# Attention on one core: the next pair's q and k turned in steps one and two, masked bias rows for each query tile

## What is computed

```python
def _fox_attend(q_blk, c_q, pos_q, k, v, c_k, pos_k):
    s = jnp.einsum('bhqd,bhkd->bhqk', q_blk, k).astype(jnp.float32) * (FOX_HEAD_DIM ** -0.5)
    s = s + (c_q[..., :, None] - c_k[..., None, :])
    s = jnp.where(pos_k[None, :] <= pos_q[:, None], s, -jnp.inf)
    p = jax.nn.softmax(s, axis=-1)
    return jnp.einsum('bhqk,bhkd->bhqd', p, v.astype(jnp.float32))
...
    o = o * jax.nn.sigmoid(gate.astype(jnp.float32))
```

## Time and profile before

| | us |
|---|---|
| median of 3 runs | 1462.0 (1460.33 to 1466.8) |
| the profiled execution, its time | 1460.39 |
| its span, first to last instruction | 1458.6 |
| PE busy in the span | 1385.2 (95%) |
| DVE, ACT, POOL busy | 532.5, 524.5, 476.3 |
| the attention steps within the span | 215.3 to about 330 |
| mean granted TensorE clock | 0.992 of full |

### The profile page before, as it was taken

One profiled execution on the slowest core, in us unless ns is written; L12 is line 12 of the kernel. 1 busy time (PEld: TensorE's weight loads), 2 busy tenths in 40 slices (PEclk: granted clock), 3 DMA queues, 4 the chain that ended last, 5 costly groups with the idle time before them and its releaser, 6 DMA issues. The chain is left out here.

```text
span 1458.6 us, 26900 instructions
## 1 busy us (share of the span) xinstructions
PE 1385.2 (95%) x11180; PEld 1037.7 (71%) x11180; DVE 532.5 (37%) x1383; ACT 524.5 (36%) x1096; POOL 476.3 (33%) x457
## 2 busy tenths in 40 slices
PE   7999998889999999999989999999999999888986
PEld 6788876567788888888867787776666665555553
DVE  3102118761312200212153613355464464444435
ACT  4325438772422222222246532333332222222222
POOL 5334546434544444444455755320000000000000
PEclk9999999999999999999999999999999999999999
DMA  5133221004232223330232131659999999999995
GB/s 187 65 111 115 88 72 47 31 16 147 84 102 71 87 87 115 116 115 15 101 124 97 58 116 59 238 196 390 403 418 420 419 420 419 420 419 420 419 419 208
DMA packets 83899, 286.49 MB, mean 196 GB/s; under 512 B 8764, under 2 KB 31456, under 8 KB 59200
## 3 DMA queue, kind: packets, MB, share of 16 engines
q1 hardware_dynamic: 83376, 283.60, 50.0%
q0 software_dynamic: 288, 1.05, 0.2%
q10 hardware_dynamic: 112, 0.09, 0.0%
HBM read 282.59 MB, written 2.13 MB: 195 GB/s over the span
## 5 line engine op out<-in xcount | busy, mean ns | idle before, releaser
L491 POOL TENSOR_TENSOR wring_halves<-wring,wring_halves 128x512 fp32r<-128x512 f32 x274 | 356.9, 1307 | 376.9 <-ACT wring_halves L486 375.1
L486 ACT CAST wring_halves<-wring 128x512 fp32r<-128x512 f32 x274 | 168.3, 621 | 433.4 <-PE ps L1207 416.6
L1205 PE MATMUL ps<-wring_halves,big_halves 128*128 128x512 f32 x612 | 241.5, 395 | 4.9 <-POOL wring_halves L491 3.8
L1205 PE MATMUL ps<-hT_halves,wring_halves 128*128 128x512 f32 x480 | 187.4, 390 | 2.4 <-DVE big_halves L1964 2.4
L1206 PE MATMUL ps<-big_halves,wring_halves 128*128 128x512 f32 x480 | 186.8, 389 | 0.0
L1207 PE MATMUL ps<-hT_halves,wring_halves 128*128 128x512 f32 x480 | 186.7, 389 | 0.0
L2654 POOL TENSOR_TENSOR rstd<-rstd,half 128x1 f32<-128x1 f32 (+1 forms) x21 | 13.6, 649 | 505.3 <-DVE rstd L2607 476.6
L1207 PE MATMUL ps<-wring_halves,hT_halves 128*128 128x512 f32 x436 | 170.6, 391 | 0.0
L1206 PE MATMUL ps<-wring_halves,hT_halves 128*128 128x512 f32 x436 | 170.6, 391 | 0.0
L1205 PEld LDWEIGHTS ps<-wring_halves,big_halves 128*128 128x128 f32 x612 | 115.4, 189 | 33.4 <-POOL wring_halves L491 7.3
L1725 PE MATMUL ps<-xn,fixed 128*128 128x512 f32 x256 | 120.0, 612 | 0.4 <-DVE fixed L2402 0.4
(11 more groups left out here) (349 smaller groups left out, 1997.5 us busy)
## 6 DMA issues: line engine op xcount, KB each, us to landing
big<-in_moe_w_dram SPq DMA_DIRECT2D x90, 1024.0 KB, 25.4
wring<-in_moe_w_dram SPq DMA_DIRECT2D x70, 1024.0 KB, 25.5
wring<-in_ffn_w_in_dram SPq DMA_DIRECT2D x22, 1024.0 KB, 7.1
hT<-in_moe_w_dram SPq DMA_DIRECT2D x20, 1024.0 KB, 25.3
wring<-in_fox_w_in_dram SPq DMA_DIRECT2D x7, 2048.0 KB, 8.7
wring<-in_gla_w_in_dram SPq DMA_DIRECT2D x6, 2048.0 KB, 7.8
mkv<-in_moe_w_dram SPq DMA_DIRECT2D x12, 1024.0 KB, 26.2
wring<-in_ffn_w_out_dram SPq DMA_DIRECT2D x4, 2048.0 KB, 7.7
```

Source lines behind the costliest of these rows:

```text
L486: act.copy(hi, src).then_inc(s_hi, 1)
L491: pool.tensor_tensor(lo, src, hi, ALU.subtract).then_inc(s_lo, 1)
L1205: pe.matmul(out, lhs[1], rhs[0], start=start, stop=False)
```

## The change

It does five things. On PE and ACT the next pair's q is turned and copied behind the transposes of step 0, and its k behind those of step 1. On ACT `out_high` moves from step 1 to step 2, and on DVE `gated` from step 0 to step 1. The bias rows are fetched as a set for each query tile: per head four transfers of 144, 272, 400 and 528 columns, where one of 528 stood. POOL masks the last 128 columns of each of the eight rows in place. And `rowmax` takes all columns up to 512 in one cut. For room, the buffers move: one set of rows starts in `arena` at column 3328, where the turned meta tokens lay, so that the first `decay_rows` waits for the last projection that reads these, and the turned probabilities of the meta keys go to `mkv`.

```diff
-        CB = L + SEQ - P
-        cbs = [arena[:, 3712:3712 + 2 * CB], wring[:, tail:tail + 2 * CB]]
-        cb = [[v[:, e * CB:e * CB + L] for e in range(2)] for v in cbs]
-        cbm = [[v[:, e * CB + L:(e + 1) * CB] for e in range(2)] for v in cbs]
+        KEYS = [META + P * (i + 1) for i in range(T)]
+        CB = sum(KEYS)
+        cbs = [arena[:, 3328:3328 + 2 * CB], wring[:, tail:tail + 2 * CB]]
+        cb = [[[v[:, e * CB + sum(KEYS[:i]):e * CB + sum(KEYS[:i + 1])] for i in range(T)] for e in range(2)] for v in cbs]
...
-        PTm = [wring[0:META, at_ptm + i * 4 * P:at_ptm + (i + 1) * 4 * P].rearrange("p (e q) -> p e q", e=2) for i in range(2)]
+        PTm = [mkv[0:META, i * 4 * P:(i + 1) * 4 * P].rearrange("p (e q) -> p e q", e=2) for i in range(2)]
...
-                    sp.dma_start(cb[p % 2][e], c_dram[h:h + 1, :].to_broadcast([P, L])).then_inc(s_cb[p % 2], 16)
+                    for i in range(T):
+                        sp.dma_start(cb[p % 2][e][i], c_dram[h:h + 1, 0:KEYS[i]].to_broadcast([P, KEYS[i]])).then_inc(s_cb[p % 2], 16)
...
+                    sp.wait_ge(s_mB, unit_of["v", 1, T] + 1)
                     decay_rows(0)
...
-                if i == 0 and p + 1 < PAIRS:
-                    qk_out(p + 1, 0)
-                if i == 1 and p:
+                if i == 2 and p:
                     out_high(p - 1)
                 pt_out(s)
-                if i == 0 and p + 1 < PAIRS:
-                    qk_out(p + 1, 1)
+                if i < 2 and p + 1 < PAIRS:
+                    qk_out(p + 1, i)
...
-                if i == 0 and p + 1 < PAIRS:
-                    qk(p + 1, 0)
                 ptrans(s)
-                if i == 0 and p + 1 < PAIRS:
-                    qk(p + 1, 1)
+                if i < 2 and p + 1 < PAIRS:
+                    qk(p + 1, i)
...
-                cuts = ([(512, n)] if n > 512 else []) + [(0, n - P), (n - P, min(n, 512))]
+                cuts = ([(512, n)] if n > 512 else []) + [(0, min(n, 512))]
...
-                if i == 0 and p:
+                if i == 1 and p:
                     gated(p - 1)
...
-                    diag = cb[p % 2][e][:, META:L].rearrange("p (t s) -> p t s", t=T)
-                    over3 = amask[:, :].unsqueeze(1).to_broadcast([P, T - 1, P])
-                    pool.tensor_tensor(cbm[p % 2][e].rearrange("p (t s) -> p t s", t=T - 1), diag[:, 0:T - 1, :], over3, ALU.add)
-                    last = pool.tensor_tensor(diag[:, T - 1, :], diag[:, T - 1, :], amask[:, :], ALU.add)
+                    for i in range(T):
+                        own = cb[p % 2][e][i][:, KEYS[i] - P:KEYS[i]]
+                        last = pool.tensor_tensor(own, own, amask[:, :], ALU.add)
```

More of the change, by code:

```diff
@@ L177, in program @@
         PT_last = [qkvg[:, :, e * D:e * D + 2 * P] for e in range(2)]
-        at_ptm = at_pt + 2 * SEQ
-        PTm = [wring[0:META, at_ptm + i * 4 * P:at_ptm + (i + 1) * 4 * P].rearrange("p (e q) -> p e q", e=2) for i in range(2)]
-        assert at_ptm + 8 * P <= W_SLOTS * 4096 + CK_SLOTS * 1024
+        PTm = [mkv[0:META, i * 4 * P:(i + 1) * 4 * P].rearrange("p (e q) -> p e q", e=2) for i in range(2)]
+        assert at_pt + 2 * SEQ <= W_SLOTS * 4096 + CK_SLOTS * 1024 and 3328 + 2 * CB <= 6144
         gateT = [xn_t[:, p * SEQ:(p + 1) * SEQ] for p in range(PAIRS)]
@@ L2065, in rowmax @@
                 n = META + P * (i + 1)
-                cuts = ([(512, n)] if n > 512 else []) + [(0, n - P), (n - P, min(n, 512))]
+                cuts = ([(512, n)] if n > 512 else []) + [(0, min(n, 512))]
                 if i == 0:
-                    dve.wait_ge(s_cb[p % 2], 32 * (p // 2 + 1))
+                    dve.wait_ge(s_cb[p % 2], 128 * (p // 2 + 1))
                     dve.wait_ge(s_cbm, p + 1)
@@ L2075, in rowmax @@
                         x = 2 * s + e
-                        d = P * i + a - (n - P)
-                        bias = cb[p % 2][e][:, a:b] if a == 0 or i == T - 1 else cbm[p % 2][e][:, d:d + b - a]
+                        bias = cb[p % 2][e][i][:, a:b]
                         last = m == len(cuts) - 1
@@ L2683, in masked_rows @@
             def masked_rows(p):
-                pool.wait_ge(s_cb[p % 2], 32 * (p // 2 + 1))
+                pool.wait_ge(s_cb[p % 2], 128 * (p // 2 + 1))
                 for e in range(2):
-                    diag = cb[p % 2][e][:, META:L].rearrange("p (t s) -> p t s", t=T)
-                    over3 = amask[:, :].unsqueeze(1).to_broadcast([P, T - 1, P])
-                    pool.tensor_tensor(cbm[p % 2][e].rearrange("p (t s) -> p t s", t=T - 1), diag[:, 0:T - 1, :], over3, ALU.add)
-                    last = pool.tensor_tensor(diag[:, T - 1, :], diag[:, T - 1, :], amask[:, :], ALU.add)
+                    for i in range(T):
+                        own = cb[p % 2][e][i][:, KEYS[i] - P:KEYS[i]]
+                        last = pool.tensor_tensor(own, own, amask[:, :], ALU.add)
                 last.then_inc(s_cbm, 1)
```

## The result

The changed kernel takes 1468.8 us (median of 5 runs, 1465.9 to 1471.9) where the kernel before takes 1462.0 (5 runs beside it, 1458.5 to 1466.8). The ratio is 1.0048, with a 95% interval of 1.0033 to 1.0064: slower by about 7 us, and outside the range of 1453 to 1466. The profiled execution took 1470.99 us, its span 1469.2.

The account below looks back on a forecast made before the run. No engine is full; a chain passing between them sets the pair. +0.2 + 2.2 - 2.6 - 1.2 = -1.4 us gave 1459.0 from the profiled execution, 1460.6 from the median; forecast 1460, range 1453 to 1466 (8 in 10).

Parts of the forecast that it names:

- The rows of the first pair: First pair's eight uncovered bias-row transfers land at 224.0 at the 189 GB/s of two transfers: 2.2 us lost.
- by packets: Upper bound for the first pair's rows: time goes by packets, four times as many, 11.6 us and 6.5 lost.
- The rows of the steady pairs: Bias rows of later pairs are covered: landed 3.3 us into the next pair, masked by 6.8, wanted at 8.6.
- The issues: SP's issuing of the bias-row transfers: two take 0.80 us, so eight take 3.2.
- the rows come late: Rival, chance 0.16: by packets, first pair loses 6.5 us, six steady pairs 0.3 each; +4.7, 1466.
- The clock: PE's clock in the attention steps: two falls kept at 1.57 us each, 0 to 4 (plus or minus 3.1 us) for the range.
- The turns: Moved q, k and out_high: pairs 1 to 6 get 0.43 us shorter (12.68), 2.6 us gained; pair 0 0.2 worse.
- The last pair: Last attention pair, with no k to copy: pv at 316.58 instead of 317.78, 1.2 us gained.
- The row maximum and `gated`: On DVE: fewer cuts save 14 us of busy time, gated goes one step later; neither gains on the path.
- `out_low` beside the normalization: POOL's out_low may hold DVE's normalization of step 3 up to 0.3 us a pair, 1.8 in all; range only.
- `wo0` issued later: SP's load of wo0 is held some 10 us by the first decay_rows; first read at 313.97, so costs nothing.
- PE as the bound: Rival, chance 0.12: k comes in time, both PE waits go, 1.9 us a pair; 1450.

Follow-up runs that it names:

- e12_alternate_timed: The changed kernel with its eight row transfers issued by query tile, the two heads alternating, semaphores and waits unchanged: 1459.6 us (12 runs), ratio 0.9975 to the kernel before.
- e11_four_copies: The changed kernel with its own issue order, but c_dram stored four times, a head's four transfers reading four copies: 1456.0 us, measured once.
- e3_split4: The kernel before with each head's bias row fetched in four transfers of 132 columns, eight transfers, same 0.54 MB: 1463.6 us, measured once.
- e1_turns: The kernel before with only the moves of q, k, out_high and gated; bias rows and row maximum as before: 1457.5 us (11 runs), ratio 0.9958.
- e4_by_tile: The changed kernel with transfers issued by query tile, heads alternating, and masking and maxima waiting for each tile by itself: 1455.9 us (10 runs), ratio 0.9958.
- e7_alternate: The changed kernel with its eight transfers issued by query tile, heads alternating, semaphores and waits unchanged: one run of 1456.1 us.
- e9_turns_old_high: The kernel before with q and k turned in steps 0 and 1 and gated in step 1, out_high left in step 1: 1464.2 us, one run.
- e8_out_high_only: The kernel before with one move alone, out_high in step 2 instead of step 1: 1459.4 us, one run.
- e2_rows: The changed kernel with the moves undone, keeping only the masked rows, eight transfers and one-cut row maximum: 1475.1 us (6 runs), ratio 1.0073.

## Why the prediction was wrong, point by point

**The rows of the first pair: wrong, and the step that decided.** I let the eight transfers run at the byte rate of two and had the last byte at 224.0, 8.6 us after the issue. It came at 227.2, after 12.0. The step that failed is "the same rate": it was measured on two transfers of different rows, and in the change four transfers after each other read the same row. Where neighbours read different rows the term was right: 8.6 us in `e12_alternate_timed`, 8.4 in `e11_four_copies`, and PE waited 2.5 and 2.2 us by it where I had 2.2. My bound of 11.6 us "by packets" was near in size (a landing at 228.3) and wrong in cause, since four times the packets landed in 6.9 us when each read its own part of the row. The Trainium skill, page "DMA: Bandwidth & Descriptors", section "Anatomy of one DMA — SWDGE (gpsimd) path", gives 2.0 us fixed for each transfer, as a fit to transfers that GpSimd issues. These come from SP, and `e3_split4` shows that no such cost is paid one after another here: its eight were issued 0.46 us apart and all had landed after 6.9. (The prediction names for this figure the section "Bandwidth", which has the advice on 1 MiB.)

**The rows of the steady pairs: wrong for the same reason.** I called them covered, landed 3.3 us into the next pair and masked by 6.8. They land 12.0 to 12.7 us after their issue instead of 8.7, and from pair 3's set on DVE waits 0.9 to 2.1 us for each. A pair without that takes 12.56 us (`e1_turns`, `e4_by_tile`). With it, it takes 12.74 to 13.35.

**The issues: too short.** 0.65 us each instead of 0.40. With the heads alternating, or with copies, 0.46 to 0.52 for the same set, and up to 0.62 for others.

**The rival "the rows come late": it should have been the forecast.** It named the place, and decides from a landing 1.4 us later than mine; it was 3.2 later. Its 6.5 us for the first pair are measured as 5.4, and its 0.3 a steady pair as 0.2 to 0.8. It gave 1466, the kernel takes 1468.8. I gave it 0.16, on the ground that two transfers ran at 189 GB/s, which says nothing of the addresses.

**The clock: three falls, inside the bounds of 0 to 4, but one of them long, and left out of the rival.** I kept two falls of 1.57 us. The steps show three stretches: 10.2 us behind PE's long wait, and 3.4 each at about 247 and 325. What the first costs comes out of the path: from the transposes of step 3 to the `pv` of step 8 it is 20.13 us (231.94 to 252.07) where it was 15.37 at full clock (226.52 to 241.89), and the moves gain 0.55 there, so the first two stretches cost 5.3 together, and the first some 3.7 if the short one costs 1.57 as in the earlier trace rows. The last one costs 1.6: the last pair takes 16.68 where 16.19 less the 1.13 gained is 15.06. Together 6.9 us, where I kept 3.1. I should have given the late rows such a price beyond the wait's own length. That long waits bring on such stretches is what these traces suggest (5.65 us ahead of 10.2, 2.46 ahead of 6.8 in `e12_alternate_timed`, 2.60 ahead of 3.4 in `e7_alternate`) and not a rule that they show: in `e11_four_copies` 2.23 us of waiting had none behind it, and before the change both falls came behind 1.3.

**The turns: right.** Pairs of 12.56 us in `e1_turns` where I had 12.68, a wait of 1.39 for k where I had 1.3, `pv` of pair 0 at 223.34 where I had 223.5. The chain of spacings ended 0.12 too late. Six pairs gain 0.55 each, 3.3 us instead of 2.6. I took `out_high` as a part of the chain and it is, at 0.52 us a pair (`e9_turns_old_high`).

**The last pair: right.** From the previous pair's last `pv` at 317.23 to its own first at 323.28 it takes 6.05 us, where 7.18 stood before (310.60 to 317.78): 1.13 gained, 1.2 forecast.

**The row maximum and `gated`: right.** DVE is busy for 11.7 us less (520.8 against 532.5; I had 14), and the time shows nothing of it: `e4_by_tile`, which has it, and `e1_turns`, which hasn't, have the same ratio of 0.9958. Moving `gated` left a pair at 13.30 us.

**`out_low` beside the normalization: too small.** I bounded it with 0.3 us a pair. In `e8_out_high_only` it costs 0.7, and the move gained nothing. In the full set of moves it is covered, which I hadn't foreseen either. The Trainium skill, page "SBUF — State Buffer", section "Who interferes with whom", says that VectorE in a 2-port mode, which a tensor_scalar can enter, and GpSimd contend for a shared pair of ports, and that whoever issues first holds it for the whole instruction. The 1.92 us beside `out_low`, against 1.20 beside `stage` and 0.90 with nothing on POOL, agree; that the 2-port mode was on, no row shows.

**`wo0` issued later: right,** as far as it can be seen: `e4_by_tile` has the same delay and the same time as `e1_turns`.

**PE as the bound: out.** Even with the k wait taken out of `pv`'s way a pair took 12.74 us, not 11.2: the next wait stood right behind it.

**The sum.** It had -1.4 us where the attention steps show +7.1, 8.5 apart. The first set lost 5.4 instead of 2.2, which is 3.2 of them. The clock cost 6.9 instead of 3.1, which is 3.8. The steady pairs gained 1.0 instead of 2.6, since DVE waited for the rows there, which is 1.6. Pair 0 and the last pair came out as forecast to 0.2.

By the steps, the sum would have been right, 1459.0, for the kernel with the rows in alternating order, which takes 1459.6. How close the two numbers are is partly luck: its runs lie between 1454.4 and 1462.0, and its profiled run has 6.8 us of low clock in the steps behind one wait, where I had counted two short falls.

## What to carry to other kernels

A byte rate read from a few transfers that read different rows needn't hold for others that reread one. So ask of several broadcasts what they read, and let consecutive ones read different rows, or wait for the part that is needed first. When a wait of PE grows, price the time that it takes, and look in the trace for low clock behind it: it stood there in the changed kernel, `e7_alternate` and `e12_alternate_timed`, and not in `e11_four_copies`. And a move in a chain between four engines is worth what the whole set leaves: `out_high` alone lost, the turns alone gained nothing, together they gave half a microsecond a pair.

## What the runs showed of the hardware

- Four consecutive broadcasts to 128 partitions that read the same DRAM row from its start (72 to 264 KB each) took 12.0 to 12.7 us for two heads in the changed kernel and 12.3 to 13.4 in `e2_rows`. The same eight with the heads alternating took 8.6 to 9.3 (`e7_alternate`, `e12_alternate_timed`), and from four copies of the table 8.3 to 8.8, once 9.6 (`e11_four_copies`). A packet cost 98 ns against 76 and 66 ns. Why rereading costs that, and whether it is the memory or the path to it, no run here tells.
- SP issued the first set of these transfers at 0.65 us each when neighbours reread a row, and otherwise at 0.40 (two transfers) or 0.46 to 0.52 (eight): an issue isn't a constant of the instruction.
- PE stood still for 5.65 us and was then granted 0.53 of its clock, the lower level of 1.2 GHz, for 10.2 us, while it was busy for 8.7 of them.
- A normalization of 2 x 528 columns on DVE took 1.92 us beside one 512-column sum on POOL (itself 1.56 instead of 1.27), 1.20 in the pairs before beside POOL's `stage`, and 0.90 with nothing on POOL.
